# Low halves of the first row quarter on GpSimd, the two high-half passes in one go on ScalarE, one ple product ahead of the router

## The chip, the cores and the metric

The kernel runs on one core of one Trainium2 chip. The engines of a core work from queues of their own and meet only in semaphores: TensorE (PE) multiplies, VectorE (DVE), ScalarE (ACT) and GpSimd (POOL) work on rows, and SyncE (SP) starts the transfers. The metric is the device time of one execution in microseconds (us), less is better. The time of a version is the median of its runs.

## What is computed

The reference is one layer of a hybrid transformer on 256 tokens of width 2048 in float32. It projects the input to queries, keys, values and gates, runs a sparse attention and an mLSTM, mixes and projects their results, normalises (the first layer norm), sends each token through two of 16 experts and adds a gated side input (`ple`), and normalises again:

```python
h = layer_norm(DN_ALPHA * h + mix @ w_out[l], ln1_g[l], ln1_b[l])
ff = hier_moe(h, w_grp[l], b_grp[l], w_exp[l], b_exp[l], w_gate[l], w_up[l], w_down[l])
ple = (p[l] @ w_ple[l]) * jax.nn.sigmoid(h @ w_ple_gate[l])
h = layer_norm(DN_ALPHA * h + ff + ple, ln2_g[l], ln2_b[l])
```

The change lies between the first layer norm and the experts. In `hier_moe` the router's logits are `xf @ w_grp` and `xf @ w_exp`; from them each token gets a group, two experts of it and their weights.

## The kernel before

Every large product up to the first norm is done in tiles of 512 columns with each factor split into a high and a low half, which take TensorE three passes. All engines' programs are straight lists of instructions, written out by hand; an engine runs its list in order, and what it must wait for is a count on a semaphore. There is no scheduler, so where an instruction stands in the code is where it runs.

The stretch that the change touches is the passage from the first norm to the experts. Its names and its steps:

- VectorE sums and normalises the 256 rows without gain and bias into `res` (written `RES`, two blocks of 128 rows; `z_ready` counts to 2). From there the rows go three ways.
- **Turned rows.** TensorE transposes `res` (`row_turn`, L858, eight of them), ScalarE and VectorE take them from PSUM with gain and bias into `h1T` (L1482, L2073), four each.
- **Router.** TensorE multiplies `h1T` with `w_router` (`router`, L868), VectorE copies the result out as `router_rows` (L2110), TensorE turns it (`router_turn`, L875), and VectorE goes through a chain of small instructions (L2114 to L2145) to `took`, which says which experts a token has (`r_took`). TensorE counts tokens per expert (`expert_counts`, L892 to L896), VectorE makes slots of the counts (L2178 to L2181) and from them the 0/1 matrix `moe_sel` (`select`, L2191, semaphore `sel_ready`).
- **Gather.** TensorE turns `moe_sel` (`row_table`, L943) and then multiplies it with the rows, which collects each expert's tokens (`first_pairs`, L959). This product takes the rows as two halves: `h1_hi`, written by ScalarE in two instructions of 128x2048 (`high(0)`, `high(1)`, L1473), and `h1_lo`, written by VectorE as `res` minus `h1_hi` in four quarters of two instructions of 128x512 each (`h1_low(q)`, L2099, semaphore `h1_lo`). `first_pairs(q)` reads quarter q of both.
- **ple products.** Between these steps TensorE does the eight products of the side input (`ple_product(n)`, L842, two matrix products of 128x512 each, shown as four matmul records), into PSUM banks 6 and 7 in turn. ScalarE copies each out to `ple_products` (`pp_copy(n)`, L1468, semaphore `pp_c`). Product n waits until copy n-2 is done.

TensorE's order there is: products 0 to 3, the eight turns, router, router turn, products 4 to 6, expert counts, product 7, a quarter of the first gate chunk (L911), the turn of `moe_sel`, the gather of pairs 0 to 3, and then the experts' first products (`up(0)`, L995). ScalarE's order is: copies 0 to 3, its turned rows, `high(0)`, copies 4 and 5, `high(1)`, copies 6 and 7, two small exponentials, and the copies of the gather. VectorE does all four quarters of the low halves after `select(0)`. GpSimd has little to do: a power for the norm (L504) and an iota (L509) just before, and then nothing until the last norm (L513).

The experts' weights come by transfers of 1 MB into a ring of eight places (`moe_ring`, L396). The first eight are loaded before the gather, every later one waits on `ring_used` until TensorE has used up the place.

## Time and profile before

| what | us |
|---|---|
| median of three runs | 1509.81 |
| lowest and highest of them | 1508.09, 1510.2 |
| the profiled execution | 1505.06 |
| span of its instructions | 1503.5 |
| TensorE busy in it | 1475.6 |
| VectorE busy | 700.3 |
| ScalarE busy | 513.4 |
| GpSimd busy | 54.8 |

The profile is of one execution, and its times are counted from the start of the span. The span ends 1.56 us short of the execution's own time. An engine's busy time says how much work it has; what holds up the end is read from the waits of the engine that is nearly always busy, here TensorE. The passage from the norm to the experts lies from 930 to 972 us.

### The profile page before, as it was taken

What the parts mean: (1) busy time and instruction counts of PE and PEld (TensorE: products, weight loads), DVE (VectorE), ACT (ScalarE), POOL (GpSimd) and SP (SyncE); (2) the same over time, 40 slices, a digit from 0 to 9 for tenths busy, and PEclk for the clock granted to TensorE, in tenths of its full rate; (3) what the DMA queues carried; (4) which work ended last, traced back from release to release, by engine and by line L of the source; (5) the groups of instructions that cost most, each with busy time, mean ns of one, the idle gap of its engine ahead of it and who ended that gap; (6) DMA issues with size and microseconds to landing.
All of it is one profiled execution on the core that took longest, in us unless ns stands there. A gap on an engine that the chain in (4) does not pass through costs nothing.

```text
span 1503.5 us, 17004 instructions
## 1 busy us (share of the span) xinstructions
PE 1475.6 (98%) x6692; PEld 1007.7 (67%) x6692; DVE 700.3 (47%) x960; ACT 513.4 (34%) x690; POOL 54.8 (4%) x63
## 2 busy tenths in 40 slices
PE   9999999999999999999999999999999998999998
PEld 7887788888788888888888887534434443454443
DVE  5546665457756554554454655531231221143336
ACT  4444444455545444344444433521000200031111
POOL 0000000044300000000000000000000000000000
PEclk9999999999999999999999999999999999999999
DMA  9654555544444555555655876599999999999995
GB/s 311 199 178 157 168 169 196 189 151 165 140 169 141 194 168 196 196 193 188 193 191 186 314 264 227 201 418 421 416 412 415 399 389 418 419 392 419 416 407 206
DMA packets 133167, 398.05 MB, mean 265 GB/s; under 512 B 13273, under 2 KB 15969, under 8 KB 108129
## 3 DMA queue, kind: packets, MB, share of 16 engines
q1 hardware_dynamic: 124352, 388.65, 69.8%
q10 hardware_dynamic: 8736, 8.33, 1.7%
q8 instruction: 52, 0.85, 0.2%
q14 instruction: 27, 0.21, 0.0%
HBM read 392.76 MB, written 4.20 MB: 264 GB/s over the span
## 4 chain that ended last, share of the span: by engine, by line
PE 92%; DMA 4%; DVE 1%; ACT 1%; issue 1%; POOL 0%; SPq 0%; DVEq 0%; POOLq 0%; ACTq 0%
PE bank L526 19%; PE bank L527 19%; PE bank L531 19%; PE bank L995 12%; PE bank L1047 5%; PE bank L911 4%; DMA moe_ring<-in_w_gate_dram 2%; PE bank L959 2%; DMA moe_ring<-in_w_ple_gate_dram 2%; PE bank L1090 1%; PE bank L1075 1%; PE bank L1091 1%; PE bank L933 1%; DMA moe_ring<-in_w_down_dram 1%; PE bank L935 1%; PE bank L934 1%
## 5 line engine op out<-in xcount | busy, mean ns | idle before, releaser
L1686 DVE TENSOR_TENSOR w_lo<-w_ring,w_hi 128x1024 fp32r<-128x1024 f32 (+1 forms) x312 | 382.0, 1226 | 300.4 <-ACT w_hi L1211 299.2
L1211 ACT ACTIVATE w_hi<-w_ring 128x1024 fp32r<-128x1024 f32 (+1 forms) x312 | 327.3, 1051 | 310.5 <-PE bank L531 307.6
L526 PE MATMUL bank<-w_hi,xT_hi 128*128 128x512 f32 (+1 forms) x864 | 346.6, 401 | 1.8 <-ACT w_hi L1211 1.8
L527 PE MATMUL bank<-w_hi,xT_lo 128*128 128x512 f32 (+1 forms) x864 | 334.9, 388 | 0.0
L995 PE MATMUL bank<-moe_ring,xg 128*64 128x512 f32 x1024 | 225.9, 594 | 8.4 <-DMA moe_ring<-in_w_gate_dram 5.8
L531 PE MATMUL bank<-w_lo,xT_hi 128*128 128x512 f32 (+1 forms) x864 | 229.3, 387 | 0.0
L526 PEld LDWEIGHTS bank<-w_hi,xT_hi 128*128 128x128 f32 x864 | 162.3, 188 | 38.0 <-issue 4.6
L527 PEld LDWEIGHTS bank<-w_hi,xT_lo 128*128 128x128 f32 x864 | 162.5, 188 | 32.3 <-issue 1.9
L531 PEld LDWEIGHTS bank<-w_lo,xT_hi 128*128 128x128 f32 x864 | 161.6, 188 | 33.1
L995 PEld LDWEIGHTS bank<-moe_ring,xg 128*64 128x64 f32 x1024 | 72.7, 137 | 154.7 <-issue 154.2
L1047 PE MATMUL bank<-moe_ring,moe_hiddenT 128*64 128x512 f32 x448 | 100.0, 595 | 1.6 <-DMA moe_ring<-in_w_down_dram 1.6
L2262 DVE TENSOR_TENSOR res<-res,bank 128x512 f32<-128x512 f32 x62 | 38.5, 681 | 103.9 <-issue 79.8
L1047 PEld LDWEIGHTS bank<-moe_ring,moe_hiddenT 128*64 128x64 f32 x448 | 31.4, 137 | 61.4 <-issue 60.2
L911 PE MATMUL bank<-moe_ring,h1T 128*128 128x512 f32 x144 | 63.4, 593 | 0.0
L2225 DVE TENSOR_TENSOR ple_sig<-bank,ple_sig 128x512 f32<-128x512 f32 x24 | 15.5, 686 | 78.9 <-PE bank L911 57.1
L526 PE MATMUL bank<-w_hi,ymT_hi 128*128 128x512 f32 x128 | 50.4, 394 | 0.0
L526 PE MATMUL bank<-w_hi,mixT_hi 128*128 128x512 f32 x128 | 50.1, 391 | 0.0
L527 PE MATMUL bank<-w_hi,ymT_lo 128*128 128x512 f32 x128 | 49.9, 390 | 0.0
L527 PE MATMUL bank<-w_hi,mixT_lo 128*128 128x512 f32 x128 | 49.8, 389 | 0.0
L526 PE MATMUL bank<-w_hi,yaT_hi 128*128 128x512 f32 x128 | 49.8, 389 | 0.0
L527 PE MATMUL bank<-w_hi,yaT_lo 128*128 128x512 f32 x128 | 49.8, 389 | 0.0
L911 PEld LDWEIGHTS bank<-moe_ring,h1T 128*128 128x128 f32 x144 | 27.2, 190 | 31.6 <-issue 31.0
(294 smaller groups left out, 1376.9 us busy)
## 6 DMA issues: line engine op xcount, KB each, us to landing
w_ring<-in_w_in_dram SPq DMA_DIRECT2D x103, 1024.0 KB, 5.0
moe_ring<-in_w_gate_dram SPq DMA_DIRECT2D x64, 1024.0 KB, 9.7
moe_ring<-in_w_up_dram SPq DMA_DIRECT2D x64, 1024.0 KB, 10.4
moe_ring<-in_w_down_dram SPq DMA_DIRECT2D x64, 1024.0 KB, 10.6
w_ring<-in_w_proj_a_dram SPq DMA_DIRECT2D x16, 1024.0 KB, 5.0
w_ring<-in_w_proj_m_dram SPq DMA_DIRECT2D x16, 1024.0 KB, 5.1
w_ring<-in_w_out_dram SPq DMA_DIRECT2D x16, 1024.0 KB, 5.1
moe_ring<-in_w_ple_gate_dram SPq DMA_DIRECT2D x15, 1024.0 KB, 12.9
```

The source lines that it names most:

```text
L526: mm(b, lh(k, m), WH[:, s, kk, 0:width], start=start and kk == 0, stop=False)
L527: mm(b, ll(k, m), WH[:, s, kk, 0:width], start=False, stop=False)
L531: last = mm(b, lh(k, m), WL[:, s, kk, 0:width], start=False, stop=stop and kk == 1)
L911: ins = mm(B[b + a][:, :], hT[:, k, a * P:a * P + P], w[:, t * NC:t * NC + NC], start=first and t == 0, stop=last and t == 3)
L933: mm(B[b + a][:, :], hTh[:, k, r], GH[:, j % 2, c], start=t == 0, stop=False)
L959: last = mm(b[:, kk * TOK:kk * TOK + TOK], src[:, a, 2 * i + kk, :], selg[:, a, :], start=part == 0 and a == 0, stop=part == 1 and a == 1)
L995: last = mm(B[b0 + i % 2][CAP * e:CAP * e + CAP, :], xg[:, k, (e0 + e) * CAP:(e0 + e) * CAP + CAP], w[e][:, t * NC:t * NC + NC], start=k = ...
L1047: last = mm(B[4 + c][CAP * e:CAP * e + CAP, :], src[:, k, CAP * e:CAP * e + CAP], w[e][:, c * NC:c * NC + NC], start=k == 0, stop=k == 3)
L1211: fn(WH[:, h % 4, :, 0:width], W32[:, h // 2, 2 * (h % 2):2 * (h % 2) + 2, 0:width], ACT.Copy).then_inc(hi_ready, 1)
L1686: v.tensor_tensor(WL[:, h % 4, :, 0:width], W32[:, h // 2, 2 * (h % 2):2 * (h % 2) + 2, 0:width], WH[:, h % 4, :, 0:width].bitcast(F32), A ...
L2225: last = v.tensor_tensor(psg[:, a, :], B[b + a][:, :], psg[:, a, :], ALU.add)
L2262: v.tensor_tensor(r, r, B[b0 + a][:, :], ALU.add).then_inc(y_add, 1)
```

## The change

Three things are done. The low halves of quarter 0 are written by GpSimd, after its iota, instead of by VectorE, with a semaphore of their own (`h1_lo_first`); VectorE keeps quarters 1 to 3, and the counts that others wait for are lowered by one. ScalarE does `high(0)` and `high(1)` one after the other and copies products 4 to 7 after both. TensorE does product 4 after the turns and ahead of the router.

```diff
@@ gpsimd
             g.iota(iota[:], pattern=[[1, CAP]], base=0, channel_multiplier=0,
                    allow_small_or_imprecise_dtypes=True).then_inc(iota_ready, 1)
+            pl.wait_ge(h1_hi, NT)
+            for a in range(NT):
+                last = g.tensor_tensor(h1l[:, a, 0:4, :].rearrange("p t q -> p q t"),
+                                       RES[:, a, :].rearrange("p (q t) -> p q t", t=KT)[:, :, 0:4],
+                                       h1h[:, a, 0:4, :].rearrange("p t q -> p q t").bitcast(F32), ALU.subtract)
+            last.then_inc(h1_lo_first, 1)
@@ tensor
             for i in range(8):
                 row_turn(i)
+            ple_product(4)
             router()
             router_turn()
-            for n in range(4, 7):
+            for n in range(5, 7):
                 ple_product(n)
@@ tensor, first_pairs
                 if q == 0:
                     pe.wait_ge(pp_c, 8)
-                pe.wait_ge(h1_lo, q + 1)
+                if q:
+                    pe.wait_ge(h1_lo, q)
+                else:
+                    pe.wait_ge(h1_lo_first, 1)
@@ scalar
             high(0)
-            pp_copy(4)
-            pp_copy(5)
             high(1)
-            pp_copy(6)
-            pp_copy(7)
+            for n in range(4, 8):
+                pp_copy(n)
@@ vector, residual
-                dv.wait_ge(h1_lo, 4)
+                dv.wait_ge(h1_lo, 3)
+                dv.wait_ge(h1_lo_first, 1)
@@ vector
-            for q in range(4):
+            for q in range(1, 4):
                 h1_low(q)
```

The order of instructions on TensorE, from the turns of the rows (`ident,res`) to the turn of `moe_sel`; `wple,pT` are the ple products (two rows of x2 to a pair of products), `h1T,w_router` the router. Before:

```order
2722 L858 MATMUL bank<-ident,res 128x128 x32
2723 L868 MATMUL bank<-h1T,w_router 32x256 x16
2724 L875 MATMUL bank<-small,router_rows 128x20 x2
2725 L842 MATMUL bank<-wple,pT 128x512 x6
2726 L892 MATMUL bank<-small,upper 128x16
```

And changed:

```order
2722 L864 MATMUL bank<-ident,res 128x128 x32
2723 L848 MATMUL bank<-wple,pT 128x512 x2
2724 L874 MATMUL bank<-h1T,w_router 32x256 x16
2725 L881 MATMUL bank<-small,router_rows 128x20 x2
2726 L848 MATMUL bank<-wple,pT 128x512 x4
2727 L899 MATMUL bank<-small,upper 128x16
```

One product (x2) has gone from the row of three behind the router turn to a place ahead of the router; two (x4) stay between the router turn and the expert counts.

The order on ScalarE, from its turned rows to the two small exponentials. Before:

```order
262 L1482 ACTIVATE h1T<-bank,small 128x256 x8
263 L1473 ACTIVATE h_hi<-res 128x128x16
264 L1468 ACTIVATE ple_products<-bank 128x512 x2
265 L1473 ACTIVATE h_hi<-res 128x128x16
266 L1468 ACTIVATE ple_products<-bank 128x512 x2
267 L1586 ACT_TABLE_LOAD
```

And changed:

```order
262 L1492 ACTIVATE h1T<-bank,small 128x256 x8
263 L1483 ACTIVATE h_hi<-res 128x128x16 x2
264 L1478 ACTIVATE ple_products<-bank 128x512 x4
265 L1594 ACT_TABLE_LOAD
```

Both high halves now stand ahead of the copies of products 4 and 5, which stood between them.

The order on GpSimd around its iota, before:

```order
39 L509 IOTA iota 128x64
40 L513 TENSOR_TENSOR small<-small 128x1 x2
41 L137 UNCONDITIONAL_BRANCH
```

And changed:

```order
39 L509 IOTA iota 128x64
40 L513 TENSOR_TENSOR h_lo<-res,h_hi 128x128x4 x2
41 L519 TENSOR_TENSOR small<-small 128x1 x2
42 L137 UNCONDITIONAL_BRANCH
```

Two instructions of 512 elements to a partition have come in behind the iota; VectorE's row of eight such instructions is one of six.

## Rows read from the trace of the kernel before

**Rows 1.** The page, busy time of each engine, its share of the span.

```profile
PE 1475.6 (98%) x6692; PEld 1007.7 (67%) x6692; DVE 700.3 (47%) x960; ACT 513.4 (34%) x690; POOL 54.8 (4%) x63
```

**Rows 2.** PE's waits from 936 to 975: us in total, times, longest us.

```profile
PE bank L868 <- DVE h1T L2073: 1.2, 1, 1.2
PE bank L875 <- DVE router_rows L2110: 0.5, 1, 0.5
PE bank L959 <- DVE h_lo L2099: 0.5, 1, 0.5
...
PE bank L959 <- ACT xg L1534: 0.3, 1, 0.3
```

**Rows 3.** Timeline of PE: start us, us, work, count, [idle before <-releaser].

```profile
937.04 3.98 PE L858 MATMUL bank<-ident,res 128*128 128x128 f32 x32 [0.29 <-DVE res L2088]
...
942.20 1.93 PE L868 MATMUL bank<-h1T,w_router 128*32 128x256 f32 x32 [1.18 <-DVE h1T L2073]
944.67 0.62 PE L875 MATMUL bank<-small,router_rows 128*128 128x20 f32 x4 [0.54 <-DVE router_rows L2110]
945.13 5.40 PE L842 MATMUL bank<-wple,pT 128*128 128x512 f32 x12
950.37 0.29 PE L892 MATMUL bank<-small,upper 128*128 128x16 f32 x2
...
951.40 1.96 PE L842 MATMUL bank<-wple,pT 128*128 128x512 f32 x4
953.20 1.88 PE L911 MATMUL bank<-ple_early,h1T 128*128 128x512 f32 x4
954.52 0.96 PE L943 MATMUL bank<-ident_r,moe_sel 128*128 128x128 f32 x4
955.92 0.48 PE L959 MATMUL bank<-moe_sel,h_hi 128*128 128x256 f32 x2 [0.45 <-DVE h_lo L2099]
```

**Rows 4.** Timeline of PE's weight loads, the first of the expert counts.

```profile
950.09 0.47 PEld L892 LDWEIGHTS bank<-small,upper 128*128 128x128 f32 x2 [0.39 <-DVE small L2145]
```

**Rows 5.** Timeline of ACT around the high halves.

```profile
941.51 3.81 ACT L1473 ACTIVATE h_hi<-res 128x2048 fp32r<-128x2048 f32 x1
947.13 0.60 ACT L1468 ACTIVATE ple_products<-bank 128x512 f32<-128x512 f32 x1 [1.81 <-PE bank L842]
...
949.34 3.74 ACT L1473 ACTIVATE h_hi<-res 128x2048 fp32r<-128x2048 f32 x1
952.87 1.13 ACT L1468 ACTIVATE ple_products<-bank 128x512 f32<-128x512 f32 x2
```

**Rows 6.** Timeline of DVE: end of the choice, the selection, the low halves.

```profile
949.78 0.26 DVE L2145 TENSOR_TENSOR small<-small 128x16 f32<-128x16 f32 x2
...
952.02 0.19 DVE L2180 TENSOR_TENSOR small<-small 128x32 f32<-128x32 f32 x1
...
952.47 1.39 DVE L2191 TENSOR_SCALAR moe_sel<-iota,small 128x64 fp32r<-128x64 f32 x8
953.77 7.97 DVE L2099 TENSOR_TENSOR h_lo<-res,h_hi 128x512 fp32r<-128x512 f32 x8
```

**Rows 7.** Groups of POOL by shape: count | busy us, mean ns | idle before.

```profile
L498 POOL TENSOR_TENSOR logits<-logits,key_mask 128x1024 f32<-128x1024 f32 x4 | 10.1, 2528 | 0.3
L498 POOL TENSOR_TENSOR logits<-logits,key_mask 128x512 f32<-128x512 f32 x4 | 5.2, 1298 | 0.3
```

**Rows 8.** Timeline of DVE, a two-input 128x512 instruction whose operands lie without gaps.

```profile
325.65 0.69 DVE L1904 TENSOR_TENSOR logits<-logits,small 128x512 f32<-128x512 f32 x1
```

**Rows 9.** Timeline of POOL, a two-input instruction beside which VectorE works.

```profile
337.74 1.30 POOL L498 TENSOR_TENSOR logits<-logits,key_mask 128x512 f32<-128x512 f32 x1
```

**Rows 10.** Timeline of DVE, two subtractions of one shape; the second meets group 9.

```profile
334.86 1.23 DVE L1686 TENSOR_TENSOR w_lo<-w_ring,w_hi 128x1024 fp32r<-128x1024 f32 x1 [0.26 <-ACT w_hi L1211]
...
338.46 1.66 DVE L1686 TENSOR_TENSOR w_lo<-w_ring,w_hi 128x1024 fp32r<-128x1024 f32 x1 [0.26 <-ACT w_hi L1211]
```

**Rows 11.** Timeline of SP: the first ring transfers behind the gather.

```profile
964.09 0.80 SPq L396 DMA_DIRECT2D moe_ring<-in_w_gate_dram  x2
```

**Rows 12.** Stretches: busy us and count by engine, PEclk, DMA share, GB/s.

```profile
970.00:1030.00 60.00, 60.00 (x258) 22.23 (x259) 13.11 (x16) 10.67 (x15) 0.00 (x0) 1.00 1.01 417
...
1275.00:1400.00 125.00, 123.21 (x565) 57.66 (x565) 37.01 (x50) 23.95 (x37) 0.00 (x0) 1.00 1.00 411
```

More of the change, by code:

```diff
@@ L296, in build @@
         wr_zero, r_part = sem("wr_zero"), sem("r_part")
-        h1_hi, h1_lo, res_gain, res_ready = sem("h1_hi"), sem("h1_lo"), sem("res_gain"), sem("res_ready")
+        h1_hi, h1_lo, h1_lo_first, res_gain, res_ready = sem("h1_hi"), sem("h1_lo"), sem("h1_lo_first"), sem("res_gain"), sem("res_ready")
         ple_in, pT_mm, pT_c, pp_mm, pp_c = sem("ple_in"), sem("pT_mm"), sem("pT_copied"), sem("pp_mm"), sem("pp_copied")
```

## The prediction

> **What bounds the kernel now.** The page's busy times come first: TensorE is busy for 1475.6 of 1503.5 us, and no other engine for half of the span [rows 1]. So an edit elsewhere pays only where TensorE waits for it. Next come TensorE's waits in the passage from the norm to the experts [rows 2], and the timelines of the engines there [rows 3 to 6]. Four waits are left for the change to win from: 1.18 us before the router for the last turned rows, 0.54 us for the copied router rows, 0.45 us before the gather for the low halves of quarter 0, and 0.3 us for a copy of the gather itself. A wait in the queue doesn't mean that filling it pays. The first is filled for nothing only with work that is no longer than it.
>
> What stands behind the gather follows it. The ring's later transfers start when the experts' first products release a place, the first at 964.09 [rows 11]. From then on TensorE is busy nearly throughout and the transfers take the whole of the DMA engines' time [rows 12]. Whichever of the two bounds a stretch there, both are started by the gather, so I pass on a shift of the gather's start, 955.92 [rows 3], to the end one for one. That is the sum to make.
>
> **Product 4 ahead of the router.** One ple product is a third of the row of twelve records: they start at 945.13 and the next work at 950.37, less about 0.08 of hand-over, which is 5.16 us for three, 1.72 each [rows 3]. Its bank has long been copied out, so it starts when the turns end, 937.04 + 3.98 = 941.02, and is through at 942.74. The router starts at 942.20 today. So 1.18 of the 1.72 us is hidden in the wait, and the router starts 0.54 later. With it the router rows, VectorE's small chain and `took` move by 0.54: `took` is ready at 949.78 + 0.26 = 950.04 today [rows 6], at 950.58 then. Today TensorE finishes product 6 at 945.13 + 5.16 = 950.29, and its weight load for the counts had waited for `took` until 950.09 [rows 4]: the two are level. With one product fewer in this place, `took` would decide alone, with 0.28 from `took` to the first product of the counts (950.37 less 950.09), thus 950.86, which is 0.49 later than today.
>
> **Both high halves in one go.** Today `high(0)` runs from 941.51 to 945.32, then ScalarE waits 1.81 us for product 4, and `high(1)` runs from 949.34 to 953.08, with the copies behind it from 952.87, 3.53 after its start [rows 5]. In the change `high(1)` starts at about 941.51 + 3.6 = 945.1 and ends at 948.9; that is a gain of 4.2 us for the high halves. The copy of product 4, now behind it, runs from about 948.7 to 949.3 instead of from 947.13 to 947.73. Product 6 needs the bank that this copy frees. Product 5 starts at 945.13 + 0.54 = 945.67 and is done at 947.39; then TensorE waits 2.06 us, to 949.45 (949.3 and a hand-over of 0.15, as from the low halves' end at 955.77 to the gather at 955.92 [rows 3, 6]). Product 6 is done at 951.17, later than `took` at 950.58 and its 0.28. So this wait decides: the counts start at 951.17 + 0.08 = 951.25, 0.88 later than today. This is the step in which the change gives back what it wins: `high(1)` takes the idle place, but the copy that TensorE needs is queued behind it.
>
> **From the counts to the gather.** Counts, product 7, a quarter of the gate chunk and the turn of `moe_sel` are TensorE's own work without a wait, from 950.37 to the turn's start at 954.52 [rows 3]; they move to 955.40. VectorE's slots and selection end at 953.86 today and at 954.74 then, 0.66 before they are needed, as today. Copies 5 to 7 are in time too, since ScalarE has nothing else to do there: product 7 is done at 954.0, its copy 0.7 later. The turn's four records take 0.95, so the gather can start at 956.35 if its inputs are there.
>
> **The low halves of quarter 0.** VectorE writes them today right after the selection, from 953.77, two instructions at 7.97 / 8 = 1.0 us each, done at 955.77; the gather had been able to start at 955.47 and waits 0.45 for them [rows 3, 6]. On GpSimd they wait for both high halves, thus start at about 949.0. No row shows this instruction on GpSimd. The nearest is its two-input work of 128x512 without gaps, 1.30 us, and of 128x1024, 2.53 [rows 7]. VectorE takes 0.69 for such operands [rows 8] and 1.0 for these, which lie in runs of four, and I carry this ratio over: 1.30 x 1.45 = 1.9 each, 3.8 for two, done at 952.9. The bounds are 1.30 from below (951.6) and twice the ratio, 3.8 each (956.6), from above. Cover is 956.35 less 949.1, 7.2 us, so up to 3.6 each it costs nothing. What is gained is the wait of 0.45, and VectorE's later work on `h1_lo` starts one quarter earlier: quarter 1 is done at about 956.6, before pairs 2 and 3, and the expert weights come earlier than TensorE asks for them, so nothing more is won there. GpSimd has nothing queued behind these two until the last norm. The wait in the rows' residual step is met in any case, since that comes some 30 us later.
>
> **The sum.** The gather starts at 956.35 instead of 955.92: +0.88 for the counts, less the 0.45 that it waits today, is +0.43 us. By the profiled execution, 1505.06 becomes 1505.5. That one lies 4.7 us under the median of the three runs; the sum doesn't depend on it, and put on the median, 1509.81, it gives 1510.2. A measurement of this kernel can tell about 0.2% from no change, 3.0 us. The change as a whole is far within it.
>
> **Rivals.** First, **the gain as meant**: the wait for copy 4 doesn't bite, because ScalarE's two instructions overlap more than I take or the product ahead of the router starts under the turns. If the router doesn't move at all and product 6 isn't held, the 0.45 us are saved: 1509.4. Against it: no more than 0.45 can come, since TensorE's own work follows without a gap from 950.37 to 955.47. A gain of over 3 us has no mechanism here; I give it only what the spread of the runs (2.1 us) can bring.
>
> Second, **VectorE and GpSimd stand in each other's way**. Where a GpSimd instruction of two inputs ran from 337.74 to 339.04, the subtraction that VectorE started at 338.46 took 1.66 us instead of 1.23 [rows 9, 10]. The two low halves would lie from 949.0 to 952.9, on top of VectorE's instructions that make `took`, which have two inputs from SBUF. If these must wait for the first of the two, `took` comes at 949.0 + 1.9 + 0.26 = 951.2, counts start at 951.5 and the gather at +0.7. If they must wait for both, `took` comes at 953.2, the counts at 953.5, the gather 3.1 less 0.45 later, +2.7: 1512.5. The Trainium skill, SBUF — State Buffer, section "SBUF: two separate sides", says that VectorE and GpSimd share a port pair as an exclusive lock, held for a whole instruction, by VectorE also where it has two SBUF inputs against a GpSimd instruction that reads SBUF. By that rule the first of these cases is what to expect; the row on 338.46 leans to it (0.43 us longer, though the whole remaining 0.58 would be expected).
>
> Third, **slower: GpSimd is slow on these runs of four**. Then its last element, not TensorE's own work, releases the gather, which starts at 949.1 + 2t + 0.1, t for one instruction. It decides from t = 3.6 on. The loss is 2t - 6.7; over 3.0 us it is from t = 4.85, 3.7 times the 1.30 of the nearest row. For it speaks only that no row shows the shape; against it that VectorE pays 1.45 for the same operands. At t = 5.5 the time would be 1509.8 + 4.3 = 1514.1.
>
> Fourth, **the change does nothing that can be seen** because the second bound of the expert stage, the transfers, absorbs the shift; then it is 1509.8, in the same class.
>
> **How the numbers follow.** Forecast, within half a microsecond of 1510.2: 0.60. Gain as meant: 0.12. Engines in each other's way, +0.7 to +2.7: 0.15. Absorbed: 0.06. GpSimd decides: 0.07, of which some 0.04 over 3 us. All but the last are within 0.2%, but the runs themselves differ by 2.1 us and the profiled one by 4.7, from which I give 0.04 to either side. So faster 0.04, same 0.88, slower 0.08. The range takes in the bounds of +2.7 over the median and, since the executions shown lie between 1505.06 and 1510.2, the forecast put on the lowest of them, 1505.5: 1505.5 to 1512.8.
>
> **What would show it right or wrong.** In the profile of the changed kernel ScalarE's two high halves stand back to back and end at about 949. TensorE has a new wait of about 2 us before the second of the two products behind the router turn, ended by ScalarE's copy; the wait of 1.18 before the router and that of 0.45 before the gather are gone. GpSimd's two instructions are under 3.6 us each. From the end of the turns to the start of the gather it is 15.3 us instead of 14.9. The forecast is wrong if TensorE waits before the counts for VectorE, or before the gather for GpSimd, or if the time moves by more than 3 us either way.

## The result, and the profile after

The changed kernel took 1512.38 us, the median of 22 runs (1508.34 to 1518.92), against 1508.33 for the kernel before beside it (22 runs, 1505.52 to 1511.73). The ratio is 1.0025, with a 95% interval of 1.0018 to 1.0033: 3.8 us slower (2.7 to 5.0). The forecast of 1510.2 was "no change", +0.43 us. The time lies in the range that was given, 1505.5 to 1512.8, and that is luck. The upper end is the kernel before at 1509.81 and +2.7 us for VectorE and GpSimd in each other's way. Beside the changed kernel the one before measured 1508.33, 1.5 us less than that, and this hid that the shift itself, 3.8 us, is larger than the +2.7 of that rival: put on 1509.81 it would be 1513.6, outside the range.

Two rows of the page of the changed kernel's profile, its span and the engines' busy times:

```profile
span 1508.2 us, 17006 instructions
PE 1477.6 (98%) x6692; PEld 1007.7 (67%) x6692; DVE 699.6 (46%) x958; ACT 513.3 (34%) x690; POOL 57.2 (4%) x65
```

Against [rows 1] TensorE has the same 6692 matmuls, yet is busy for 2.0 us more. This is the first thing to see: the work did not grow, its matmuls ran longer. GpSimd has the two instructions that it was given, 2.4 us more in all. The span is 4.7 us longer, 1508.2 against 1503.5.

TensorE's waits of the changed kernel, 936 to 975 (us in total, times, longest us), answer to [rows 2]:

```profile
PE bank L848 <- ACT ple_products L1478: 1.7, 1, 1.7
PE bank L899 <- DVE small L2154: 1.0, 1, 1.0
...
```

The wait of 1.18 before the router and that of 0.45 before the gather are gone, as forecast. Two stand in their place: one for the copy of product 4, as forecast, and one for `took` (L2154), which the forecast had only in a rival.

Timeline of TensorE in the changed kernel (start us, us, work, count, [idle before <-releaser]); it answers to [rows 3]:

```profile
936.95 3.97 PE L864 MATMUL bank<-ident,res 128*128 128x128 f32 x32 [0.29 <-DVE res L2097]
940.76 1.88 PE L848 MATMUL bank<-wple,pT 128*128 128x512 f32 x4
942.57 1.93 PE L874 MATMUL bank<-h1T,w_router 128*32 128x256 f32 x32
...
949.23 1.98 PE L848 MATMUL bank<-wple,pT 128*128 128x512 f32 x4 [1.75 <-ACT ple_products L1478]
952.18 0.40 PE L899 MATMUL bank<-small,upper 128*128 128x16 f32 x2 [0.97 <-DVE small L2154]
...
953.32 3.38 PE L848 MATMUL bank<-wple,pT 128*128 128x512 f32 x4
...
958.13 0.96 PE L950 MATMUL bank<-ident_r,moe_sel 128*128 128x128 f32 x4
958.93 0.45 PE L966 MATMUL bank<-moe_sel,h_hi 128*128 128x256 f32 x2
```

I measure from the start of the turns (936.95 here, 937.04 before), so that what lies ahead of the passage drops out. The counts start 15.23 us after it instead of 13.33: +1.90. From the counts to the turn of `moe_sel` it is 5.95 instead of 4.15: +1.80. From that turn to the gather it is 0.80 instead of 1.40: -0.60. The gather comes 21.98 us after the turns' start, not 18.88: **+3.10**, where the forecast had +0.43.

Product 7 is the row to look at. Its four matmuls take 3.38 us and took 1.96 before, with no wait in them. The granted clock tells why. Stretches of the changed kernel (TensorE's busy us and count, PEclk, DMA share, GB/s):

```profile
953.00:954.00 1.00, 1.00 (x7) 0.86 0.00 0
954.00:955.00 1.00, 1.00 (x3) 0.50 0.00 0
...
957.00:958.00 1.00, 1.00 (x3) 0.93 0.00 0
```

From about 953.7 to 957.1 TensorE was granted half of its full speed, 1.2 GHz instead of 2.4, in a stretch where it was busy throughout. Before it stood the two new waits, 1.75 and 0.97 us, with 1.98 us of work between. The Trainium skill, "TensorE: Matmul & The Clock Gate", section "Why this matters for your kernels", warns of idle gaps between bursts of matmuls that bring the clock to its half, but of gaps longer than either of these. Here two shorter gaps, close to each other, were followed by it, so the page's advice alone would have passed them, and the measurement decides.

ScalarE, GpSimd and VectorE of the changed kernel in the same passage, one timeline each (columns as above); they answer to [rows 5] and [rows 6]:

```profile
941.42 7.33 ACT L1483 ACTIVATE h_hi<-res 128x2048 fp32r<-128x2048 f32 x2
948.52 1.13 ACT L1478 ACTIVATE ple_products<-bank 128x512 f32<-128x512 f32 x2
```

```profile
948.83 2.98 POOL L513 TENSOR_TENSOR h_lo<-res,h_hi 128x512 fp32r<-128x512 f32 x2 [14.43 <-ACT h_hi L1483]
```

```profile
948.79 0.17 DVE L2129 COPY small<-small 128x2 f32<-128x2 f32 x1
...
949.26 0.18 DVE L2128 MAX8 small<-small 128x8 f32<-128x16 f32 x1
949.48 0.90 DVE L2129 COPY small<-small 128x2 f32<-128x2 f32 x1
...
950.49 0.16 DVE L2130 MATCH_REPLACE8 small<-small 128x16 f32<-128x16 f32 x1
950.68 1.15 DVE L2152 TENSOR_SCALAR small<-small 128x8 f32<-128x8 f32 x1
951.87 0.26 DVE L2154 TENSOR_TENSOR small<-small 128x16 f32<-128x16 f32 x2
```

The high halves stand back to back and end at 948.75. GpSimd's two low halves run from 948.83 to 951.81. Within that time two tiny instructions of VectorE take 0.90 and 1.15 us; the same COPY took 0.17 when it started just before GpSimd did. Both end when one of GpSimd's two ends (about 950.3 and 951.8). Not every instruction is held: MAX8 at 949.26 and MATCH_REPLACE8 at 950.49 ran beside GpSimd and kept their 0.18 and 0.16. So `took`, which stood behind them, came 1.71 us later than this chain of VectorE alone would have it, and part of that was covered by the wait for copy 4.

### The profile page after: what moved, and what is told of

The parts are those of the page before. It is cut to its first block, busy times and chain, and to the rows that moved or that the text cites. A ratio compares the mean times of both kernels' runs of the same rounds, so it can differ in the third digit from the quotient of the medians.

```text
span 1508.2 us, 17006 instructions
## 1 busy us (share of the span) xinstructions
PE 1477.6 (98%) x6692; PEld 1007.7 (67%) x6692; DVE 699.6 (46%) x958; ACT 513.3 (34%) x690; POOL 57.2 (4%) x65
## 4 chain that ended last, share of the span: by engine, by line
PE 92%; DMA 4%; DVE 1%; ACT 1%; issue 1%; POOL 0%; SPq 0%; DVEq 0%; POOLq 0%; ACTq 0%
PE bank L532 19%; PE bank L533 19%; PE bank L537 19%; PE bank L1005 12%; PE bank L1057 5%; PE bank L918 5%; DMA moe_ring<-in_w_gate_dram 2%; PE bank L966 2%; DMA moe_ring<-in_w_ple_gate_dram 2%; PE bank L1100 1%; PE bank L1085 1%; PE bank L1101 1%; DMA moe_ring<-in_w_down_dram 1%; PE bank L940 1%; PE bank L941 1%; PE bank L942 1%
```

## The experiments

**What is disputed.** The passage gained three lumps: the copy behind both high halves, VectorE held while GpSimd works, and the fall of the clock. My theory after the first profile was that the three are separate, that the waits bring the fall, and that GpSimd's work matters only as what makes the second wait. The rivals were that GpSimd's work itself brings the fall or takes longer than it shows, that the high halves alone cost the time, and that what lies behind the gather, which differs from execution to execution, made the difference. In all experiments "the passage" is the time from the start of the turns to the start of the gather, 18.88 us in the kernel before.

### The low halves back on VectorE

The changed kernel with its GpSimd part taken out:

```diff
-            pl.wait_ge(h1_hi, NT)
-            for a in range(NT):
-                last = g.tensor_tensor(h1l[:, a, 0:4, :].rearrange("p t q -> p q t"),
...
-            last.then_inc(h1_lo_first, 1)
...
-            for q in range(1, 4):
+            for q in range(4):
                 h1_low(q)
```

> The changed kernel with the low halves of quarter 0 on VectorE again; the high halves in one go and product 4 ahead stay. Theory A, GpSimd holds up VectorE's chain to took by 1.7 us: without it took is ready at 950.4 instead of 952.1 and the counts start when product 6 is done, 951.0 to 951.1. TensorE waits 1.75 us before product 6 and nothing before the counts. If the clock stays up with this one wait, the gather starts at 956.6, when VectorE is done with quarter 0, and the time is 0.7 us over before; if it falls, 1.7 more. Rival B, VectorE's chain was late for another reason: took stays at 952.1 and the counts at 952.2.

Measured: ratio 1.0005 (0.9994 to 1.0016); the passage is 19.66 us, +0.78. TensorE's and VectorE's timelines of this kernel:

```profile
949.23 1.98 PE L842 MATMUL bank<-wple,pT 128*128 128x512 f32 x4 [1.74 <-ACT ple_products L1469]
951.05 0.29 PE L893 MATMUL bank<-small,upper 128*128 128x16 f32 x2
...
955.20 0.96 PE L944 MATMUL bank<-ident_r,moe_sel 128*128 128x128 f32 x4
956.62 0.47 PE L960 MATMUL bank<-moe_sel,h_hi 128*128 128x256 f32 x2 [0.46 <-DVE h_lo L2098]
```

```profile
949.49 0.17 DVE L2119 COPY small<-small 128x2 f32<-128x2 f32 x1
```

The wait for copy 4 is the same (1.74), the instructions of VectorE take 0.17 again, the second wait is gone, and from counts to turn it is 4.15 as before the change. The counts come 0.76 later than before the change: this is the whole price of copy 4's new place together with the router, forecast at 0.88. The other 1.14 of the counts' 1.90 belongs to GpSimd's part. The wait of 0.46 before the gather is back.

### The GpSimd part alone

The kernel before, with the low halves of quarter 0 on GpSimd and nothing else changed:

```diff
+            pl.wait_ge(h1_hi, NT)
+            for a in range(NT):
+                last = g.tensor_tensor(h1l[:, a, 0:4, :].rearrange("p t q -> p q t"),
...
+            last.then_inc(h1_lo_first, 1)
...
-            for q in range(4):
+            for q in range(1, 4):
                 h1_low(q)
```

> The kernel before with only the GpSimd part. GpSimd's two instructions now start behind the second high half, at about 953.0, beside VectorE's selection (952.47 to 953.86), not beside the chain to took. Theory A, they hold up VectorE's one-input instructions on SBUF operands: the selection's remaining instructions wait for GpSimd's, it ends at about 956 or later, and the gather starts at about 957, 1 to 1.5 us later than before. Rival B, only instructions with two SBUF inputs are held up: the selection ends at 953.9, the gather starts when GpSimd is done, at 956.1 to 956.2, and the time is 0.2 to 0.3 us over before. In both no wait before the counts and the clock at 1.00.

Measured: ratio 1.0012 (1.0002 to 1.0022); passage 19.93, +1.05. Here the high halves end late, so GpSimd meets VectorE's selection. Timelines of this kernel, VectorE, GpSimd and TensorE:

```profile
952.95 3.95 DVE L2201 TENSOR_SCALAR moe_sel<-iota,small 128x64 fp32r<-128x64 f32 x8
```

```profile
953.66 3.03 POOL L513 TENSOR_TENSOR h_lo<-res,h_hi 128x512 fp32r<-128x512 f32 x2 [18.68 <-ACT h_hi L1482]
```

```profile
956.95 0.66 PE L949 MATMUL bank<-ident_r,moe_sel 128*128 128x128 f32 x4 [1.39 <-DVE moe_sel L2201]
```

The eight instructions of the selection take 3.95 us and took 1.39 [rows 6]; their end follows GpSimd's by 0.2, and TensorE waits 1.39 us for them. So the hold-up is not bound to one instruction or to `took`: it strikes COPY and TENSOR_SCALAR wherever they meet GpSimd. GpSimd's own time hardly changes (3.03 and 2.98 for two).

### Both new waits filled with matmuls

The changed kernel, with matmuls that nothing uses put where TensorE waits:

```diff
+            def filler(count):
+                for _ in range(count):
+                    mm(B[1][:, :], pT[:, 0, 0:P], wple[:, 0, 0:NC], start=True, stop=True)
...
-            for n in range(5, 7):
-                ple_product(n)
+            ple_product(5)
+            filler(2)
+            ple_product(6)
+            filler(1)
```

> The changed kernel, with TensorE's two new waits filled by products that nobody reads (two before product 6, one before the counts, 0.86 us each, into a bank that is free). Theory A, the clock: the granted clock fell to half from about 953.9 to 957.1 in the changed kernel because TensorE had idled before; kept busy, it stays at 1.00, counts still start at about 952.2 (GpSimd's work still holds up VectorE), and the turn of moe_sel starts some 4.15 us behind them instead of 5.95. The gather is 1.8 us earlier than in the changed kernel, 957.2, and the time about 1.8 us lower. Also, the runs scatter less than the changed kernel's 1508 to 1519. Rival B, the clock fell for another reason (the GpSimd work, chance): it falls here too, and the gather stays at 959.

Measured: ratio 1.0013 (1.0002 to 1.0024); passage 20.33, +1.45. TensorE's timeline:

```profile
953.10 0.40 PE L905 MATMUL bank<-small,upper 128*128 128x16 f32 x2
...
957.35 0.96 PE L956 MATMUL bank<-ident_r,moe_sel 128*128 128x128 f32 x4
```

The counts come as late as in the changed kernel (15.28 us after the turns' start, 15.23 there), and VectorE is held in the same way. But from the counts to the turn it is 4.25 us, not 5.95, and the granted clock stays at 1.00. GpSimd runs beside it as before. So GpSimd's work alone doesn't bring the fall, and 1.65 to 1.8 of the passage's 3.10 us hang on the fall. That TensorE's idle time brings it is what this profile suggests; one profile without a fall doesn't show it, as the two of one kernel further below will make plain.

### The high halves in one go, alone

```diff
             high(0)
-            pp_copy(4)
-            pp_copy(5)
             high(1)
-            pp_copy(6)
-            pp_copy(7)
+            for n in range(4, 8):
+                pp_copy(n)
```

> The kernel before with only ScalarE's part, both high halves ahead of copies 4 to 7. By the prediction's step product 6 waits for copy 4 from 948.57 to about 949.3, the counts start at 951.0 to 951.1, 0.7 later than before, and so does the gather, 956.6. The clock stays at 1.00, since TensorE waits only 0.7 us longer: time 0.7 us over before. If the clock falls here too, it is the passage's low work as such and not the two longer waits that bring it down, and the time is 1.5 to 2 us more.

Measured: ratio 1.0008 (0.9999 to 1.0017); passage 19.70, +0.82. TensorE's timeline:

```profile
950.47 1.98 PE L842 MATMUL bank<-wple,pT 128*128 128x512 f32 x4 [0.53 <-ACT ple_products L1468]
952.29 0.29 PE L892 MATMUL bank<-small,upper 128*128 128x16 f32 x2
```

The counts come 0.80 later than before the change, as with the product ahead of the router (0.76). Whether product 4 stands ahead of the router or behind it makes no difference to the counts, since the late copy decides in both. Nor does it change how long TensorE idles: with product 4 behind the router it waits 1.18 before the router and 0.53 for the copy, with it ahead nothing and then 1.74. Product 4 ahead of the router has joined two short waits into one long one and done nothing else.

### The changed kernel again, on another chip

No edit.

> The changed kernel itself once more, with its own profile. If the fall of the granted clock in its first profile comes from TensorE's two waits (1.75 and 0.97 us), it comes again: a stretch of about 3.4 us at 0.50 somewhere between 952 and 962, and the time between the counts' start and the turn of moe_sel is well over 4.15 us. If it hung on chance alone, it needn't. GpSimd's two instructions hold up the same two instructions of VectorE, 0.7 and 1.0 us. Time 0.2 to 0.3% over before.

Measured: ratio 1.0008 (0.9997 to 1.0018), 1510.12 against 1508.88. That is lower than the 1.0025 of the result, and the two intervals only touch. Its profile shows the same passage, 22.00 us against 21.98. One stretch of it:

```profile
954.00:955.00 1.00, 1.00 (x3) 0.51 0.00 0
```

So the passage repeats to 0.02 us, the fall included, and yet the timed runs are nearer to those of before: 1.2 us (-0.5 to 2.7), where 3.1 in every execution would lie outside. So the fall was probably not in all of them. What follows tests that.

### Product 6 behind the counts

A different cure: the kernel before, with the product that has to wait put behind the counts.

```diff
-            for n in range(4, 7):
+            for n in range(4, 6):
                 ple_product(n)
...
             expert_counts()
+            ple_product(6)
             ple_product(7)
```

> The kernel before with product 6 moved behind the expert counts and nothing else: no GpSimd work, ScalarE's order as before. TensorE then waits about 1.5 us for took between product 5 and the counts. With the clock up, counts start at 950.3, the turn of moe_sel 1.72 later than before at 956.2 and the gather at 957.15: time 1.2 us over before. Theory A, waits in this passage bring the clock down: then a stretch at 0.50 behind the counts and up to 1.7 us more. Rival B, a single wait of 1.5 us is not enough (in the kernel with low halves on VectorE one of 1.74 was not): clock at 1.00.

Measured: ratio 1.0019 (1.0009 to 1.0028); passage 19.82, +0.94.

```profile
950.13 0.40 PE L892 MATMUL bank<-small,upper 128*128 128x16 f32 x2 [1.28 <-DVE small L2146]
...
956.10 0.96 PE L943 MATMUL bank<-ident_r,moe_sel 128*128 128x128 f32 x4
```

TensorE waits 1.28 us for `took`, the counts come only 0.27 earlier, and the whole product of 1.72 then lies on the path. In the kernel before, product 6 was free, because it filled the time until `took`.

### GpSimd beside the router's chain

The kernel before, with one of the two blocks of quarter 0 on GpSimd, at an earlier place, where VectorE makes the router's choice:

```diff
+            pl.wait_ge(h1_hi, 1)
+            for a in range(1):
+                last = g.tensor_tensor(h1l[:, a, 0:4, :].rearrange("p t q -> p q t"),
...
+            last.then_inc(h1_lo_first, 1)
...
-                for a in range(NT):
+                for a in range(NT) if q else (1,):
```

> The kernel before, in which GpSimd writes the first block of quarter 0's low halves right after the first high half, from about 945.4 to 946.9, beside the start of VectorE's chain to took; VectorE writes only the second block. Theory A, a GpSimd instruction holds up VectorE's next one-input instruction between SBUF operands until it ends: the small copy at 945.63 takes about 1.2 instead of 0.17 us, took comes 1.0 later, counts start at 951.4, the gather at 956.5, 0.6 later than before. Rival B, only two-input instructions are held up, of which the first comes at 947.4: nothing moves, the low halves of quarter 0 are done 1 us sooner and the gather starts at 955.5, 0.45 earlier than before.

Measured: ratio 1.0003 (0.9993 to 1.0013); passage 19.24, +0.36. GpSimd and VectorE of this kernel:

```profile
945.56 1.51 POOL L513 TENSOR_TENSOR h_lo<-res,h_hi 128x512 fp32r<-128x512 f32 x1 [10.92 <-ACT h_hi L1481]
```

```profile
945.78 1.31 DVE L2124 COPY small<-small 128x8 f32<-128x8 f32 x1
```

One COPY takes 1.31 instead of 0.17 us and ends with GpSimd's instruction (947.07 and 947.09). One instruction of GpSimd, 1.51 us long, has cost the router's chain 1.14. The counts come 0.86 later by it, and 0.5 of that comes back before the gather.

### The filler split: the first wait, the second wait

The same matmuls at one of the two places only:

```diff
             ple_product(5)
             filler(2)
             ple_product(6)
-            filler(1)
```

> The changed kernel with only the wait before product 6 filled (two products of 0.86 us that nobody reads), GpSimd's work unchanged. One wait of about 1.0 us is left before the counts, which start at 952.2. If it takes both waits to bring the clock down: clock at 1.00, turn 4.15 behind the counts, gather at 957.2 to 957.3. If the wait right before the counts is enough: a stretch at 0.50 and the gather at 959.

```diff
             ple_product(5)
-            filler(2)
             ple_product(6)
             filler(1)
```

> The changed kernel with only the wait before the counts filled (one product of 0.86 us that nobody reads), GpSimd's work unchanged. The wait of 1.75 us before product 6 stays, that before the counts is about 0.3. If it takes both waits: clock at 1.00, as in the version with the low halves on VectorE, which had the first wait alone; gather at 957.2 to 957.3. If GpSimd's work or the first wait is what counts: a stretch at 0.50 and the gather at 959.

Measured: 1.0019 (1.0010 to 1.0028) and 1.0011 (1.0002 to 1.0021); passages 20.33 and 20.31. TensorE's timeline with the first wait filled:

```profile
952.37 0.40 PE L905 MATMUL bank<-small,upper 128*128 128x16 f32 x2 [1.00 <-DVE small L2160]
...
956.62 0.96 PE L956 MATMUL bank<-ident_r,moe_sel 128*128 128x128 f32 x4
```

and with the second filled:

```profile
950.15 1.98 PE L848 MATMUL bank<-wple,pT 128*128 128x512 f32 x4 [1.74 <-ACT ple_products L1484]
```

In both profiles the clock stays at 1.00 through the passage and 4.25 us lie between counts and turn. One profile each is in line with a fall that takes both waits together; it isn't proof of it.

### Both waits without GpSimd

The counterpart: the waits kept, GpSimd idle. Low halves on VectorE, quarter 0 ahead of what makes `took`:

```diff
             best(1, 2, me, r1)
+            h1_low(0)
             experts_one_hot()
...
-            for q in range(4):
+            for q in range(1, 4):
                 h1_low(q)
```

> As the version with the low halves on VectorE, but VectorE writes quarter 0's two low halves (2 x 1.0 us) inside its chain, just ahead of took. GpSimd does nothing here, yet took is 2.0 us late, at about 952.35, and TensorE has both waits of the changed kernel: 1.74 us before product 6 and about 1.3 before the counts. Theory A, the two waits bring the clock down: a stretch of about 3.4 us at 0.50 behind the counts, and the turn of moe_sel some 5.9 us behind the counts' start instead of 4.15; the gather at about 959.3. Rival B, GpSimd's work has to do with the fall: clock at 1.00 here, gather at 957.6.

> The version of the changed kernel in which VectorE, not GpSimd, makes took late, looked at a second time. Its first profile had both waits (1.75 and 1.17 us) and no fall of the clock, while its runs had a mean granted clock of 0.9968, like the changed kernel's and 0.001 under the kernel before. If TensorE's waits bring the clock down in most executions but not in all, this look may show the stretch at 0.50 behind the counts, with the turn 5.9 us behind the counts' start. A second look without a fall makes GpSimd's part in it more likely, and leaves that open.

Measured: ratio 1.0020 (1.0011 to 1.0029). The first profile, TensorE:

```profile
950.43 1.98 PE L842 MATMUL bank<-wple,pT 128*128 128x512 f32 x4 [1.75 <-ACT ple_products L1469]
953.59 0.40 PE L893 MATMUL bank<-small,upper 128*128 128x16 f32 x2 [1.17 <-DVE small L2144]
...
954.73 1.96 PE L842 MATMUL bank<-wple,pT 128*128 128x512 f32 x4
...
957.84 0.96 PE L944 MATMUL bank<-ident_r,moe_sel 128*128 128x128 f32 x4
```

and the second profile of the very same kernel, its timeline and a stretch (busy us and count of PE, PEld, DVE, ACT, POOL, then PEclk, DMA share, GB/s):

```profile
949.63 1.98 PE L842 MATMUL bank<-wple,pT 128*128 128x512 f32 x4 [1.74 <-ACT ple_products L1469]
952.80 0.40 PE L893 MATMUL bank<-small,upper 128*128 128x16 f32 x2 [1.18 <-DVE small L2144]
...
953.93 2.95 PE L842 MATMUL bank<-wple,pT 128*128 128x512 f32 x4
...
958.75 0.96 PE L944 MATMUL bank<-ident_r,moe_sel 128*128 128x128 f32 x4
```

```profile
956.00:958.00 2.00, 2.00 (x4) 0.84 (x3) 2.00 (x5) 1.06 (x2) 0.00 (x0) 0.50 0.00 0
```

The ratio is that of the first measurement; the second is a single execution of 1513.64 us, beside 1506.59 for the kernel before. The waits are equal to 0.01 us in the two profiles. In one the clock held and product 7 took 1.96 us, in the other it fell and product 7 took 2.95, with 5.95 us from counts to turn. GpSimd had no work here. So the fall needs no GpSimd, and the waits **allow** it rather than force it: it comes in some executions of one kernel and not in others. That also limits the steps above: one profile each does not settle whether a single one of the two waits is enough. What can be said is the count over all 14 profiles: a fall in this passage in three of the four with both waits (the changed kernel twice, this one once), and in none of the ten others, five of which have one wait of 1.0 to 1.8 us behind the router. Chance would put all three falls on those four in about one case of 90.

### Blocks moved by halves: a version that should win

The kernel before, with the first half of product 4 (1.0 us, less than the wait of 1.18) ahead of the router and the second behind the router turn, half of the gate chunk's rows ahead of the counts, and block 0 of the low halves ahead of VectorE's slots:

```diff
+            ple_product(4, (0,))
             router()
             router_turn()
-            for n in range(4, 7):
+            ple_product(4, (1,))
+            for n in range(5, 7):
                 ple_product(n)
+            early_rows(0)
...
             distances()
+            h1_low(0, (0,))
             slots()
             select(0)
+            h1_low(0, (1,))
```

> A version meant to beat both: no GpSimd work, ScalarE's order as before. TensorE does only the first half of product 4 (0.86 us) in the wait before the router, and one half of the gate chunk's first quarter before the counts, so that it has 0.86 us less to do behind them; VectorE writes the first block of quarter 0's low halves in its own wait for the counts. Router and counts start when they did, at 942.2 and 950.4, the turn of moe_sel at 954.0 instead of 954.5, the gather at 955.0 instead of 955.9. Time 0.9 us under before, which is less than the runs scatter by; the clock stays at 1.00. If VectorE's extra instruction or the copies on ScalarE come in late, it shows as a wait before the turn or the gather and the gain is less.

Measured: ratio 0.9995 (0.9986 to 1.0004). The passage is 17.94 us, 0.94 shorter. TensorE's timeline (the turns start at 937.98):

```profile
951.31 0.29 PE L901 MATMUL bank<-small,upper 128*128 128x16 f32 x2
...
955.92 0.47 PE L968 MATMUL bank<-moe_sel,h_hi 128*128 128x256 f32 x2 [0.36 <-DVE h_lo L2106]
```

The trace shows the gain where it was expected: a piece no longer than the wait is free, and the counts do not move (13.33 us after the turns' start in both). The time shows none that can be told from nothing. So this version has not been shown to beat the kernel before.

## What the timed runs add: the clock as a term

A fall of the clock that comes in some executions only can't be read from one profile. But every timed run comes with the mean granted clock of its execution. From it follows a bound on what falls cost: 1 less that mean, times 1508 us. It is a bound, because the clock also falls where nothing depends on it. In every profile it is at half at the end, when TensorE has no work left. A stretch of the kernel before, behind TensorE's last products, which end at 1497.5:

```profile
1500.00:1504.00 4.00, 0.00 (x0) 0.55 0.25 90
```

In this profile all that the clock falls short by, 1.6 us, lies there. Over the 14 profiles the end alone accounts for 0.9 to 2.8 us. The difference to the kernel before takes it out only on the average.

I took this term only after I had seen the runs, so it is a reading and no test. The mean clock of the kernel before fell short of 1 by 0.0022 to 0.0023 in three measurements; for those beside the first measurement of the changed kernel no clock is on record, and 0.0022 is taken there too. The standard error of such a difference is about 0.0003, or 0.5 us. "Passage" is the difference of the passage, in the changed kernel and its repetition without the 1.80 of the fall, which the clock term already holds.

| kernel | 1 - clock | clock term, us | passage, us | sum | measured, us (95%) |
|---|---|---|---|---|---|
| changed | 0.0035 | 1.8 | 1.3 | 3.1 | 3.8 (2.7 to 5.0) |
| changed again | 0.0026 | 0.5 | 1.3 | 1.8 | 1.2 (-0.5 to 2.7) |
| low halves on VectorE | 0.0027 | 0.6 | 0.8 | 1.4 | 0.8 (-0.9 to 2.4) |
| GpSimd part alone | 0.0026 | 0.5 | 1.0 | 1.5 | 1.8 (0.3 to 3.3) |
| both waits filled | 0.0023 | 0.0 | 1.4 | 1.4 | 2.0 (0.3 to 3.6) |
| high halves alone | 0.0029 | 1.0 | 0.8 | 1.8 | 1.2 (-0.2 to 2.6) |
| product 6 behind the counts | 0.0030 | 1.2 | 0.9 | 2.1 | 2.9 (1.4 to 4.2) |
| GpSimd beside the router's chain | 0.0028 | 0.9 | 0.4 | 1.3 | 0.5 (-1.1 to 2.0) |
| first wait filled | 0.0032 | 1.5 | 1.4 | 2.9 | 2.9 (1.5 to 4.2) |
| second wait filled | 0.0027 | 0.7 | 1.4 | 2.2 | 1.7 (0.3 to 3.2) |
| both waits without GpSimd | 0.0032 | 1.4 | 1.6 | 3.1 | 3.0 (1.7 to 4.4) |
| moved by halves | 0.0023 | 0.0 | -0.9 | -0.9 | -0.8 (-2.1 to 0.6) |

Every sum lies within its measured interval. The intervals are about 3 us wide, so this is a weak agreement: the passage alone, without the clock term, lies within 8 of the 12 intervals. The kernel with both waits filled is the only one with the changed order whose clock is that of the kernel before, but it stands only one standard error from the changed kernel's repetition. Two things stay open. Which falls make up the clock term can't be said from the mean: later places have one too. TensorE's timeline and a stretch of the changed kernel's repetition, far behind the passage:

```profile
1451.56 0.47 PE L940 MATMUL bank<-gate_hi,h1T_hi 128*128 128x512 f32 x1 [2.17 <-DVE gate_lo L2292]
```

```profile
1452.00:1454.00 2.00, 2.00 (x8) 0.59 1.03 430
```

In the kernel before the wait at the same place is 2.06 us and the clock stays at 1.00.

That wait, which the change doesn't touch, was followed by a fall in five of the profiles (low halves on VectorE, high halves alone, GpSimd beside the router's chain, product 6 behind the counts, changed again) and by none in the others. The length of the wait doesn't tell them apart: 2.04 to 2.18 us in the five, 2.06 to 2.40 in the others. Two more places have a fall in some profiles: about 1385, behind a single wait of 2.46 and of 2.04 us (high halves alone, GpSimd beside the router's chain), and about 1135, behind a wait of 2.22 us that had one of 1.31 ahead of it, with 3.65 us of work between (second profile of both waits without GpSimd). A stretch of the kernel with the high halves alone:

```profile
1380.00:1390.00 10.00, 7.54 (x27) 0.83 1.01 420
```

So a fall doesn't need two waits everywhere in this kernel; that it took both in the passage is as far as the profiles go. And part of each clock term may be from these places or from the end. "First wait filled" leaves it open: its profile has no fall while TensorE works, and its runs have 1.5 us in the mean. And why the two measurements of the changed kernel differ, 0.0035 and 0.0026, is not known; they were taken on different chips, and no run tells the chip from chance.

## Where the prediction was right and where it was wrong

By its own signs the forecast was wrong, although its time fell into the range: TensorE waits before the counts for VectorE, and the time moved by 3.8 us (2.7 to 5.0), where 3 was the limit. From the end of the turns to the gather it is 18.0 us, not 15.3. Two steps failed, named below.

**What bounds the kernel**: right. TensorE is busy for 98% in both, and each change of the passage could be read from its waits.

**Product 4 ahead of the router**: right. The router starts 5.62 us after the turns' start instead of 5.16, +0.46 for the +0.54 forecast.

**Both high halves in one go**: right in mechanism, nearly in size. ScalarE's two stand back to back and end at 948.75 (forecast 948.9); product 6 waits 1.75 for 2.06; the counts come 0.76 later by this alone for 0.88. The miss is that `high(1)` and the copy came 0.1 to 0.2 sooner than assumed.

**Low halves on GpSimd, their own time**: 1.51 each, forecast 1.9 within 1.30 to 3.8. The ratio 1.45 that VectorE pays didn't carry over; GpSimd paid 1.51 / 1.30 = 1.16. The forecast had the operands wrong as well: only `res` is read in runs of four, `h1_hi` and `h1_lo` are taken with a step of 128 elements. It cost nothing here, since the cover was 3.6 each. The third rival, GpSimd as the one that decides, is out.

**GpSimd beside VectorE: the first step that failed.** The sum put nothing for it, and rival two had it at 0.15. It named "two inputs from SBUF" as what is held and took [rows 9, 10] as its measure, 0.43 us. It also said that by the page's rule the first case was to be expected, and still left it out of the sum and gave the rival 0.15; nothing in the rows is a reason for that. In the runs, one-input instructions between SBUF operands were held (COPY and TENSOR_SCALAR), and for all of the rest of GpSimd's instruction: 0.90 and 1.15 in place of 0.17 each. Its case for "both" had the counts at 953.5; they came at 952.18, since GpSimd was faster than assumed. In kind this rival came true. Its price, from 1.90 less 0.76, is 1.14 us on the counts. The Trainium skill, "SBUF — State Buffer", section "SBUF: two separate sides", states the lock also for VectorE's one-input instructions in its fast modes; I had used the half on two inputs alone. The traces here agree with the wider rule: COPY and TENSOR_SCALAR were held, MAX8 and MATCH_REPLACE8 were not. No two-input instruction of VectorE ran beside these of GpSimd in the changed kernel, so that half stays as [rows 9, 10] have it.

**From the counts to the gather: the second step that failed, and the largest.** "They move to 955.40" took the 4.15 us as a block. It is TensorE's own work without a wait, but its length is not a constant: it took 5.95, at half the clock, behind the idle time that now stood ahead of it. I had worked out both waits, 2.06 from the sum and the one for `took` in the rival, and weighed their length but never what two of them in a row do to the clock. With them filled it was 4.25. The same two waits left it at 4.25 in one profile of another kernel too, so the term is one with a chance, about 1.8 us in some executions.

**The wait of 0.45 before the gather**: right, gone, and with it 0.15 more.

**One for one to the end**: neither shown nor refuted. From the gather to the end of the span it was 547.6 in the profile before and 549.3 in that of the changed kernel, and over all kernels 547.6 to 552.6, in no order that follows the passage. The profile before was at the low end of this, so a comparison of the two profiled executions (1505.06 and 1509.71) overstates what can be assigned. The table's sums, which pass the shift on one for one, fit.

**The sum.** Forecast +0.88 - 0.45 = +0.43. The passage has +0.76 + 1.14 - 0.60 = +1.30 without a fall and +3.10 with one. The forecast's chance of 0.08 for slower by over 0.2% (3.0 us) met a result of 3.8 (2.7 to 5.0), which lies about at that bound; the repetition gave 1.2 (-0.5 to 2.7). That the change doesn't help is settled. Whether it is beyond 3 us isn't.

## What to carry to other kernels

Fill a wait of TensorE with a piece that is no longer than the wait, and then follow each queue on which the moved work had stood: here the copy behind the second high half was late, and the product pulled forward only joined two waits into a longer one. Add up the idle time that a change leaves on TensorE ahead of a dense stretch, and count a clock term for it with a chance, even if each wait alone looks small and is paid by nothing on the path. Work given to an idle GpSimd must lie where VectorE has nothing to do that anyone waits for: price each GpSimd instruction that a COPY or TENSOR_SCALAR of the chain meets at what is left of it.

## What the runs showed of the hardware that was not expected

COPYs of 128x2 and 128x8 and a TENSOR_SCALAR of 128x8, 0.17 us each, took 0.90 to 1.31 us beside a GpSimd instruction between SBUF operands, and ended with it; MAX8 and MATCH_REPLACE8 of 128x16 kept their 0.18 and 0.16 beside it. GpSimd's own instructions took 1.51 to 1.57 us in all of these kernels.

The granted clock fell to 0.50 for about 3.4 us, in a stretch where TensorE was busy, after two waits of 1.75 and 0.97 to 1.18 us with 1.98 us of work between them, in three of four profiles. It cost 1.7 to 1.8 us. The same kernel with the same waits kept its clock in one execution and lost it in another. Later in the kernel a single wait of 2.04 to 2.46 us was followed by a fall in some profiles and by none in others.

GpSimd's low halves took 1.51 us each at 128x512, with `res` in runs of four and the other two operands with a step of 128 elements, against 1.30 without gaps; VectorE's ratio for the same is 1.0 against 0.69.
